# GpSimd left idle: weight remainders on VectorE, a convolution and the adaptive modulation reshaped on TensorE

## What is computed

```python
mod = silu(c) @ ada_w + ada_b                 # 1024 x 6144, one row c
sh1, sc1, g1, sh2, sc2, g2 = split(mod, 6)
h = rmsnorm(x, norm_mix_w) * (1 + sc1) + sh1
hq, hf, hi, hg, sq, sk, sv, iq, ik, iw, cu = split(h @ w_in)
o_a = hgrn2_mixer(hq, hf, hi, hg, ...)        # gated recurrence, by decay levels
o_b = dsa_mixer(sq, sk, sv, iq, ik, iw)       # top-64 keys of an index score, then softmax
o_c = conv_module(cu, cv_w, cv_b, ...)        # a*sigmoid(b), 31-tap causal depthwise conv, LayerNorm, swish
x = x + g1 * (concat(o_a, o_b, o_c) @ w_out)
h = rmsnorm(x, norm_mlp_w) * (1 + sc2) + sh2
x = x + g2 * (square(relu(h @ mlp_w1)) @ mlp_w2)
x = rmsnorm(x, final_norm_w)
for i in range(2):                            # layer 0: latent + stick-breaking attention; layer 1: forgetting attention
    x = layer_norm(ALPHA * x + mixer(x)); x = layer_norm(ALPHA * x + swiglu(x))
    x = x + sigmoid(x @ ple_w_gate[i] + ple_b_gate[i]) * (p[i] @ ple_w_proj[i])
```

## Time and profile before

| | us |
|---|---|
| median of 3 runs | 1412.34 |
| span of the profiled execution, first to last instruction | 1405.2 |
| TensorE matmul busy | 1200.8 |
| VectorE busy | 727.2 |
| ScalarE busy | 521.1 |
| GpSimd busy | 813.5 |

### The profile page before, as it was taken

How to read it: one execution, slowest core, us unless ns; L and a number is a source line. 1 busy time by engine, 2 the same in 40 slices (tenths; PEclk the granted TensorE clock), 3 DMA queues, 4 the chain that set the end, 5 groups by cost and what they waited for, 6 DMA issues and landing times.

```text
span 1405.2 us, 18835 instructions
## 1 busy us (share of the span) xinstructions
PE 1200.8 (85%) x8000; PEld 1104.7 (79%) x8000; DVE 727.2 (52%) x778; ACT 521.1 (37%) x672; POOL 813.5 (58%) x225
## 2 busy tenths in 40 slices
PE   6699769576999996975779999976999788999976
PEld 5699658466998885973679999866987488999866
DVE  2396999656999005336555553074022536555054
ACT  1453210433343333456433333333554433333341
POOL 0476896133877882740157878844743146888863
PEclk9899879868999997997799999988999889999998
DMA  9442218412444554330034455524432033455540
GB/s 363 167 175 90 91 36 302 172 44 106 164 167 174 185 183 161 139 129 1 31 120 150 181 180 182 207 92 165 181 120 90 0 120 130 191 186 184 181 148 30
DMA packets 28131, 200.95 MB, mean 143 GB/s; under 512 B 3089, under 2 KB 3473, under 8 KB 4881
## 3 DMA queue, kind: packets, MB, share of 16 engines
q1 hardware_dynamic: 26624, 190.30, 37.0%
q10 hardware_dynamic: 1424, 9.46, 1.8%
HBM read 198.70 MB, written 1.05 MB: 142 GB/s over the span
## 4 chain that ended last, share of the span: by engine, by line
PE 68%; DVE 20%; ACT 5%; issue 4%; DMA 1%; POOL 1%; DVEq 0%; ACTq 0%; POOLq 0%
PE bank L491 19%; PE bank L496 18%; PE bank L497 18%; PE bank L569 6%; DVE hT_hi L1344 4%; DVE hT_lo L1345 3%; DVE arena L1677 2%; PE bank L620 2%; DVE hid_lo L1679 2%; DVE arena L1529 1%; PE bank L613 1%; DVE hid_hi L1678 1%; PE bank L857 1%; PE bank L856 1%; POOL w_lo L1279 1%
## 5 line engine op out<-in xcount | busy, mean ns | idle before, releaser
L1279 POOL TENSOR_TENSOR w_lo<-raw,w_hi 128x2048 fp32r<-128x2048 f32 (+1 forms) x159 | 731.3, 4600 | 569.6 <-PE bank L491 489.2
L949 ACT ACTIVATE w_hi<-raw 128x2048 fp32r<-128x2048 f32 (+1 forms) x159 | 299.6, 1886 | 342.1 <-PE bank L491 288.2
L491 PE MATMUL bank<-hT_hi,w_hi 128*128 128x256 f32 (+1 forms) x1360 | 392.1, 288 | 35.1 <-DVE hT_lo L1345 30.1
L496 PE MATMUL bank<-hT_lo,w_hi 128*128 128x256 f32 (+1 forms) x1360 | 389.3, 286 | 0.0
L497 PE MATMUL bank<-hT_hi,w_lo 128*128 128x256 f32 (+1 forms) x1360 | 389.1, 286 | 0.0
L491 PEld LDWEIGHTS bank<-hT_hi,w_hi 128*128 128x128 f32 (+1 forms) x1360 | 264.3, 194 | 39.7 <-DVE hT_lo L1345 20.3
L496 PEld LDWEIGHTS bank<-hT_lo,w_hi 128*128 128x128 f32 (+1 forms) x1360 | 264.2, 194 | 0.2
L497 PEld LDWEIGHTS bank<-hT_hi,w_lo 128*128 128x128 f32 (+1 forms) x1360 | 263.7, 194 | 0.3
L491 PE MATMUL bank<-w_hi,hT_hi 128*128 128x256 f32 (+2 forms) x544 | 164.5, 302 | 35.0 <-DVE hT_lo L1345 29.0
L496 PE MATMUL bank<-w_lo,hT_hi 128*128 128x256 f32 (+2 forms) x544 | 161.8, 298 | 0.0
L497 PE MATMUL bank<-w_hi,hT_lo 128*128 128x256 f32 (+2 forms) x544 | 161.7, 297 | 0.0
(11 more groups left out here) (242 smaller groups left out, 1347.0 us busy)
## 6 DMA issues: line engine op xcount, KB each, us to landing
raw<-wstream SPq DMA_DIRECT2D x179, 1024.0 KB, 4.8
arena<-prow ACTq DMA_DIRECT2D x2, 2560.0 KB, 8.9
x_res<-x ACTq DMA_DIRECT2D x1, 1024.0 KB, 12.4
rows<-prow ACTq DMA_DIRECT2D x2, 512.0 KB, 15.4
out<-x_res SPq DMA_DIRECT2D x1, 1024.0 KB, 4.0
const_sb<-const ACTq DMA_DIRECT2D x1, 936.0 KB, 14.2
raw<-wstream SPq DMA_DIRECT2D x1, 768.0 KB, 4.1
raw<-wstream SPq DMA_DIRECT2D x1, 544.0 KB, 3.6
```

Source lines behind the costliest of these rows:

```text
L491: ins = mm(o, a[0], b[0], start=start, stop=False)
L496: mm(o, a[0], b[1], start=False, stop=False)
L949: A(w_hi[n % HI][:, 0:m], raw[:, slot % RAW, 0:m], ACT.Copy).then_inc(weights_rounded, 1)
L1279: nc.gpsimd.tensor_tensor(w_lo[n % LO][:, 0:m], raw[:, slot % RAW, 0:m], w_hi[n % HI][:, 0:m].bitcast(F32), ALU.subtract).then_inc(weights ...
```

## The change

GpSimd gets no work. (1) The remainder is computed by VectorE, in `lo_ahead`, called at hand-chosen places of VectorE's order, and it is written over the raw tile: `w_lo` are views of `raw`, of which there are five. A raw slot is loaded again when TensorE has begun the tile after the one in it. (2) The convolution is 62 float32 matmuls of 128x256 with diagonal matrices of the taps, which VectorE and ScalarE make at the start (31 each, of 128x128), into two banks that ScalarE reads with the bias. (3) The modulation uses 32 columns of the array for each matmul: four row blocks k go to four column groups and leave four partial rows in one bank; VectorE copies the bank out, and a further matmul with a matrix of ones at rows 0, 32, 64 and 96 adds them (`modulation_sum`), which now stands between the modulations. (4) The identity is loaded ahead of the input by a DMA of its own.

```diff
-RAW, HI, LO = 3, 3, 2
+RAW, HI = 5, 3
...
+        w_lo = [nc.alloc_sbuf_tensor_at(f"w_lo{i}", [P, TILE], F32R, offset=raw_at + 4 * i * TILE) for i in range(RAW)]
...
@@ sync
                 if i >= RAW:
                     before = STREAM[i - RAW]
-                    if before in SPLIT_NO:
-                        sp.wait_ge(weights_split, SPLIT_NO[before] + 1)
+                    if before == "hi.1":
+                        sp.wait_ge(psum_full, full("hi", 1))
+                    elif before in SPLIT_NO:
+                        sp.wait_ge(weights_started, SPLIT_NO[before] + 2)
                     elif int(before[3:]) % 2 == 0:
                         sp.wait_ge(ada_used, int(before[3:]) // 2 + 1)
...
@@ tensor, modulation
-                    for k in range(DC):
-                        last = mm(b[:, j * T:(j + 1) * T], csil[:, k:k + 1].to_broadcast([P, P]), w[:, k, :],
-                                  start=k == 0, stop=k == DC - 1)
+                    for half in range(2):
+                        for g in range(4):
+                            k = 4 * half + g
+                            last = mm(b[32 * g:32 * g + 32, j * T:(j + 1) * T],
+                                      csil[:, k:k + 1].to_broadcast([P, 32]), w[:, k, :],
+                                      start=half == 0, stop=half == 1)
                     last.then_inc(psum_full if j else ada_used, 1)
+            def modulation_sum(u):
+                in_sbuf("mod", u)
+                b = begin("ms", u)
+                part = lev_tmp[u % 2]
+                if u in (4, 5, 10, 11):
+                    last = mm(b[:, :], pick_row, part, start=True, stop=True)
+                else:
+                    for c in range(4):
+                        last = mm(b[:, c:c + 1], part[:, c * P:(c + 1) * P], pick_row[:, 0:1],
+                                  start=True, stop=True)
+                last.then_inc(psum_full, 1)
+            def modulations(first, end):
+                for u in range(first, end + 1):
+                    if u < end:
+                        modulation(u)
+                    if u > first:
+                        modulation_sum(u - 1)
...
             decay_level(0)
             decay_level(1)
+            pe.wait_ge(taps_made_dve, 1)
+            pe.wait_ge(taps_made_act, 1)
+            in_sbuf("cu", 0)
+            for c in range(2):
+                b = begin("conv", c)
+                for j in range(31):
+                    last = mm(b[:, 0:T], tap_matrix(c, j), hpad[:, c * 286 + j:c * 286 + j + T],
+                              start=j == 0, stop=j == 30)
+                last.then_inc(psum_full, 1)
             gemm_feature("sqk")
...
-            for u in range(4, N_ADA // 2):
-                modulation(u)
+            modulations(4, N_ADA // 2)
...
@@ scalar
+            for j in range(31):
+                last = A(tap_matrix(1, j), ident, ACT.Copy, scale=col("cv_w", 2 * j + 1))
+            last.then_inc(taps_made_act, 1)
             act.wait_ge(norm_coef_ready, 1)
...
             decay_exp(1)
             decay_exp(2)
+            for c in range(2):
+                b = wait_full("conv", c)
+                done(A(conv[:, c * T:(c + 1) * T], b[:, 0:T], ACT.Identity, bias=col("cv_b", c)), "conv", c)
...
-        @block.gpsimd
...
@@ vector
+            def lo_ahead(name, by=1, last=len(SPLIT) - 1):
+                while next_lo[0] <= min(SPLIT_NO[name] + by, last):
+                    n = next_lo[0]
+                    m, slot = width(SPLIT[n]), TILE_NO[SPLIT[n]] % RAW
+                    dve.wait_ge(weights_rounded, n + 1)
+                    V.tensor_tensor(w_lo[slot][:, 0:m], raw[:, slot, 0:m], w_hi[n % HI][:, 0:m].bitcast(F32),
+                                    ALU.subtract).then_inc(weights_split, 1)
+                    next_lo[0] += 1
...
+            for j in range(31):
+                last = V.tensor_scalar(tap_matrix(0, j), ident, col("cv_w", 2 * j), None, ALU.mult)
+            last.then_inc(taps_made_dve, 1)
             rms_norm(1)
...
+            lo_ahead("hf.0", 0)
             split_transposed("mix")
             for j in range(2):
+                lo_ahead(f"hf.{j}")
                 wait_done("hf", j)
...
             for j in range(2):
+                lo_ahead(f"hq.{j}")
                 b = wait_full("hq", j)
...
+            lo_ahead("cu.0")
             dve.wait_ge(logs_done, 1)
...
+            lo_ahead("cu.1")
             wait_done("cu", 1)
...
+            lo_ahead("idx")
             decay_factors(1)
             for lv in range(2, 9):
                 if lv + 1 <= 8:
                     decay_args(lv + 1)
+                if lv in (3, 5, 7):
+                    lo_ahead({3: "sqk.1", 5: "hg.1", 7: "hi.1"}[lv], last=SPLIT_NO["hi.1"])
                 decay_factors(lv)
...
+            for u in range(4, 13):
+                if u < 12:
+                    modulation_part(u)
+                if u > 4 and u - 1 in gate_rows:
+                    modulation_row(u - 1, gate_rows[u - 1])
+                elif u > 4:
+                    modulation_columns(u - 1)
...
+            lo_ahead("hi.1", 2)
             softmax("dsa", 4, 0, lambda t: sel_bias[t][:, 0:(t + 1) * P], 0.125, 4)
...
             for n in range(16):
                 key = (f"m1_{n // 2}", n % 2)
+                lo_ahead(f"m1_{n // 2}.{n % 2}")
                 wait_done(*key)
...
+            for q in range(16):
+                lo_ahead(f"m2_{q}")
             gated_residual2()
...
+                    lo_ahead("ff")
...
+                    lo_ahead("fv0.1")
...
                 layer_norm(0, 1, f"ln1_{layer}", layer)
                 for i in range(11):
+                    lo_ahead(f"f13_{layer}_{i}.0")
                     b0 = wait_full(f"f13_{layer}_{i}", 0)
...
+                    lo_ahead(f"f13_{layer}_{i}.1")
                     b1 = wait_full(f"f13_{layer}_{i}", 1)
...
+                for i in range(11):
+                    lo_ahead(f"f2_{layer}_{i}")
...
                 layer_norm(2, 3, f"ln2_{layer}", layer)
                 for n in range(4):
                     key = (f"pg{layer}_{n // 2}", n % 2)
+                    lo_ahead(f"{key[0]}.{key[1]}")
```

More of the change, by code:

```diff
@@ L163, in psum_plan @@
 def psum_plan():
-    plan = [("mod", u) for u in range(4)]
+    plan = []
+    def modulations(first, end):
+        for u in range(first, end + 1):
+            if u < end:
+                plan.append(("mod", u))
+            if u > first:
+                plan.append(("ms", u - 1))
+    modulations(0, 4)
     def transposes(stage):
@@ L184, in psum_plan @@
     level(1)
+    plan.extend([("conv", c) for c in range(2)])
     gemm("sqk")
@@ L195, in psum_plan @@
     plan.extend([("sc", t, j) for t in range(TT) for j in range(4)])
-    plan.extend([("mod", u) for u in range(4, N_ADA // 2)])
+    modulations(4, N_ADA // 2)
     plan.extend([("hgo", 0), ("hgo", 1)])
@@ L283, in rounded @@
             return nc.alloc_sbuf_tensor_at(name, [P, n], F32R, offset=arena_at + 4 * offset)
-        raw = sb("raw", [P, RAW, TILE])
         w_hi = [rounded(f"w_hi{i}", TILE) for i in range(HI)]
-        w_lo = [rounded(f"w_lo{i}", TILE) for i in range(LO)]
+        w_lo = [nc.alloc_sbuf_tensor_at(f"w_lo{i}", [P, TILE], F32R, offset=raw_at + 4 * i * TILE) for i in range(RAW)]
         x = sb("x_res", [P, TT, D])
@@ L636, in _ @@
             pe.wait_ge(c_ready, 1)
-            for u in range(4):
-                modulation(u)
+            modulations(0, 4)
+            pe.wait_ge(ident_loaded, 16)
             pe.wait_ge(const_loaded, 16)
@@ L1381, in softmax @@
                 for i in range(n + 3):
+                    if name == "fox" and 1 <= i <= 6:
+                        lo_ahead(f"{FOX_UPPER[i - 1][0]}.{FOX_UPPER[i - 1][1]}")
                     if i < n:
@@ L1437, in _ @@
             V.memset(hpad, 0.0)
+            link(V.memset(pick_row, 0.0))
+            for g in range(4):
+                V.memset(pick_row[32 * g:32 * g + 1, :], 1.0)
             link(V.memset(ones[:, :], 1.0))
@@ L1766, in _ @@
                 if layer == 0:
+                    lo_ahead("cqkv.0")
                     wait_done("cqkv", 0)
+                    lo_ahead("cqkv.1")
                     wait_done("cqkv", 1)
@@ L1779, in _ @@
                     V.memset(suffix_mask, 1.0)
+                    lo_ahead("kr")
                     b = wait_full("kr")
@@ L1801, in _ @@
                     own(k_rope_ready)
+                    lo_ahead("sbv.1")
                     for j in range(2):
@@ L1808, in _ @@
                     n = len(us)
+                    lo_ahead("ukv", 0)
                     for i in range(n):
```

106 lines of the change are left out of this document (49 added, 57 removed).

## The result

The changed kernel takes 1398.82 us (median of 4 runs, 1396.19 to 1400.31) against 1412.53 us (1410.88 to 1413.70): a ratio of 0.9906, 95% interval 0.9891 to 0.9921. It is 13.7 us faster, not the 34 forecast, and falls 1.8 us outside the range.

What follows compares the result with a forecast made beforehand. GpSimd, on nobody's chain, was taken to delay VectorE, which ends TensorE's waits. Terms 1 to 6 and wo0 (+6.2) and the rest (-40.3) gave -34.1: 1405.2 to 1371.1, with 7.1 around it 1378 us; range 1358 to 1397.

Steps and rivals of the forecast that it cites:

- term 7: First tiles of later stages: TensorE's mid-tile waits on GpSimd-blocked split casts shrink or vanish, from -1.1 to -6.9 us each.
- m1 and m2: VectorE needs 5.0 of 5.76 us per tile, so the two stages take 180.8 us for 192.9: -12.1.
- Start: Up to the input products: ada tiles become load-bound, coefficients at 36.4, products at 42.5 us; -12.0 (-6 to -14).
- Input products: VectorE's order stalls hq.1 by 2.6 and sv by 4.1 us, plus one partly cold resumption; +7.8 (0 to +10).
- Decay stage: Convolution adds 27.2 us on TensorE, remainders and exponentials wait in order; +15.4 us (-10 to +20).
- Rival (c): TensorE is the bound of the decay stage, which takes about 79 us; 1353 us, chance 0.12.
- To the wo0 casts: After the search: modulation sum waits for VectorE's copy, leaving nine loads of 2.8 us still to come; +13.5 (+10 to +17).
- Rival (b): Every stall of TensorE resumes at half clock, some 13 stalls of 1.6 us, 3 counted; 1396 us, chance 0.08.
- The constant: Time around the profiled span of 1405.2 us up to the median 1412.3, taken as 7.1 us and added to 1371.1.
- (a): Modulation column groups run one after another, tiles at 3.5 us after the search; 1396 us, chance 0.12.
- (d): In-place subtraction costs VectorE what it costs GpSimd, 4.6 us for a remainder; slower, 1455 us, chance 0.04.
- (e): The blocks are not GpSimd's doing, only added work stays and the 40.3 us vanish; 1418 us, chance 0.03.

Runs made afterwards that it cites:

- subtraction_alone: Changed kernel with only the subtraction moved to VectorE, convolution on GpSimd and modulations 128 columns wide as before; 1399.95 us, ratio 0.9906 to the kernel before.
- wide_modulations: Changed kernel with modulations again 128 columns wide, with no copy and no sum after them; 1399.07 us, ratio 0.9915 to the kernel before.
- one_tap: Changed kernel with 30 of the 31 tap products of each convolution half left out on TensorE; 1375.76 us, ratio 0.9767 to the kernel before.
- early_subtractions: Changed kernel with VectorE's subtractions called earlier in its own order; 1350.92 us, ratio 0.9594 to the kernel before.
- sums_after_search: Changed kernel with products of modulation units 4 to 8 run before the first sum, the others interleaved; 1382.54 us, ratio 0.9800 to the kernel before.
- half_and_half: Changed kernel with early subtractions, late modulation sums, and the convolution's channels split between TensorE and GpSimd; 1322.17 us, ratio 0.9381 to the kernel before.

## Why the prediction was off, point by point

In the spans the forecast missed 25.6 us (-34.1 against -8.5). Of these 20.0 lie in term 7 with the stretch of the fox stage (-34.2 forecast, -14.2 measured), 3.4 in the start, 2.7 in the loads to wo0, 2.6 in the input products and the decay stage; m1 and m2 gave 2.7 more than forecast, and the softmax row 0.3.

**What bound the kernel**: right. GpSimd blocked VectorE, and `subtraction_alone` gets the whole gain by ending that.

**Start (-12.0, measured -8.6).** The wait for the first split fell from 12.05 to 3.02 us, as said. Mis-sized was the point at which the coefficients stand, 39.8 us for 36.4. The last ada tile is there at 34.0 for 33, and the price of 0.88 us for it and about 1 for the sum was that of the full clock, while this stretch ran at half:

```profile
16.00:40.00 24.00, 17.04 (x116) 10.87 (x117) 5.33 (x13) 12.82 (x38) 0.00 (x0) 0.50 1.02 419
```

The tile takes 1.93 us, the last sums, 16 records of two units, 3.57, and the transposes after them 3.65. In `wide_modulations` TensorE works from 9.1 to 39.5 us without a gap, the granted clock of this window is 1.00, and the same transposes take 1.91. Between 16 and 40 us the clock falls to 0.50 in every trace with column groups, and in none of the three without. So the groups save work under the loads, lose clock by it, and shorten the start by only 1.4 us.

**Input products (+7.8, measured +8.6).** Stalls of 2.4 and 3.7 us where 2.6 and 4.1 were worked out, each followed by a tile of about 7.5 us for 5.76. Right, as far as one trace can tell (other traces have the stage at 69.1 us, as said above).

**Decay stage (+15.4, measured +17.2).** Right in size and in its items: the convolution 27 (`one_tap`: 27.5), hg.1 3.3 for 4.1, hi.1 4.4 for 6.2. Rival (c), TensorE as the only bound, did not hold; the 95.2 us of `early_subtractions` show what the order of the remainders had cost.

**Search (-17.1, measured -17.2).** Right.

**To the wo0 casts (+13.5, measured +16.2).** The mechanism was right and `sums_after_search` shows it. A load took 2.69 us (VectorE's last copies follow each other by 5.36, a pair), less than the 2.8 taken. What was too small was the delay before them: the last of the nine lands 31.3 us after the search, so 7.1 us pass beside the nine loads, where 3.4 were taken; the sum goes first on TensorE, 2.07 us, and only the tile after it frees a buffer.

**Two remainders ahead of the softmax (+4.6, measured +4.3)**: right.

**First tiles.** wo0, o0 and o1 gave -5.4, -4.6, -5.5 for -6.0, -5.7, -6.0. The step that failed is the same term at the others: cqkv, the two pg, ff and the second f13 were to give -14.3 together and gave +2.9, of which 6.0 belong to the next paragraph. I let the gap of before vanish where nothing else was late, and took the next remainder as less late than it was. In the trace cqkv's first tile is 6.1 us earlier, but sbq.0 stalls 1.5 and uq 2.6 us on their remainders, and the stretch keeps 2.4. At pg the stall on the remainder (3.7 and 4.7 us) replaces the stall on the split (3.5 and 3.4), so nothing is gained for the -2.5 and -1.1. At ff 1.7 and 1.9 replace 4.5. `early_subtractions` shows that these were the price of VectorE's order, not of the work: the same subtractions, called during the product before, made the two pg stretches 6.8 and 6.3 us shorter.

**The last attention: 0 in the forecast, +6.0 within the +4.6 of its row.** I had put the fox stage at nothing because its remainders lie in waits. They do; what differs is the clock after two pauses that are the same in both kernels. Whether the change did this is open: the trace of before took 5.3 us less than that kernel's median, so other executions of it may well have had such falls, and no trace shows those. Rival (b) had the rule, but tied it to the stalls that the change makes; it also strikes pauses that were there before.

**m1 and m2 (-12.1, measured -14.8)**: right. The sum of the tiles, 180.8 us, is what the changed kernel took (180.8). The row of before that I set it against ended 2 us too early.

**The constant (7.1 us).** Wrong, and it flattered the forecast. Only 1.8 us lie around the span; the other 5.3 are how far the traced execution of before fell short of the median. They made a miss of 25.6 us in the span look like one of 20.4 in the difference of the medians. That the number came within 2 us of the range is in that part luck.

**The rivals.** (a) is out: a tile takes 0.97 us at the full clock for 3.57, and 1.93 at half. (b) holds in part: a stall at pg cost 6.3 to 6.8 us for 3.7 to 4.7, one at f13 about itself. (c), (d) and (e) are out, by the 105.7 us, the 2.29 us and the casts of 428 ns. The measured number is near that of (a) and (b), both 1396, though (a) did not happen and (b) only at some stalls. The range took in both and ended 2 us too low.

**What stays open.** Why the convolution on TensorE and on GpSimd come out equal both with late and with early subtractions (2.7 us apart with early ones, and 3.2 us of the difference of those two traces lie in the last attention, where the clock decides) may be chance of sizes; `half_and_half` shows only that half of each costs less than all of either. Why the same pause drops the clock in one trace and not in another was not tried beyond filling it.

## What to carry to other kernels

When work moves to an engine whose program has one fixed order, its duration is the smaller question; price where each piece stands in that order, and call it while the engine waits for the product before. Here that was worth 44 to 48 us, where the change brought 13.7. Before a trace is read as typical, compare its execution with the others: here it was 5.3 us short of the median. A wait for an engine that is in a long stretch of its own (the search) stops all that is queued behind it, loads included: run first what doesn't need it. And when two places for the same work each cost what the other saves, try half in each.

## What the runs showed of the hardware

- Pauses of 1.09 us of TensorE were followed by some 6 us at 1.2 GHz in some executions of the same instructions and not in others, at 3.0 us each (6 us in two cases); four 128x128 float32 products ahead of the wait removed it. It moved up to 6 us between kernels that differ elsewhere.
- VectorE's two-input operations of 128x512 beside GpSimd's taps of 128x512 took 1.5 us for 0.69, beside taps of 128x256 1.0 to 1.2 us (the timeline of `half_and_half` has 1.02 at 105.47 and 1.21 at 106.41), in turns with them.
- Four column groups of 32 ran side by side in float32: 0.97 us for a tile at the full clock, against 3.57 in the full width; 1.93 at half.
- Less work on TensorE under a load-bound stretch also meant a lower clock: 0.50 from 16 to 40 us with the column groups, and 16 transposes in 3.65 us for 1.91.
